# Attention passes of a hybrid layer: projecting queries and keys by tokens and transposing them, instead of projecting by features

## The chip, the cores and the metric

The kernel runs on one core of a Trainium2 chip. Five engines have queues of their own and meet through semaphores: the matrix engine (PE in the profile, with its weight loads as PEld), the vector engine (DVE), the scalar engine (ACT), GpSimd (POOL) and the sync engine (SP), which here issues the weight transfers. The metric is the device time of one execution in microseconds, the median of several.

## What is computed

One encoder layer on 256 tokens of width 2048: a projection feeds latent attention (16 heads) and a matrix-memory recurrence (8 heads), both are merged, and cross-attention and a gated feed-forward block with convolution follow. The change touches the latent attention and the convolution of the recurrence's queries and keys.

```python
def rms_norm(x, g):
    y = x * lax.rsqrt(jnp.mean(x * x, axis=-1, keepdims=True) + EPS)
    return y * g
def apply_rope(x, cos, sin):
    x1, x2 = x[..., :half], x[..., half:]
    return jnp.concatenate([x1 * cos - x2 * sin, x2 * cos + x1 * sin], axis=-1)
...
    q = (rms_norm(z_qa, g_qa) @ w_qb).reshape(b, s, 16, 128 + 64)
    kv = (rms_norm(z_kv, g_kva) @ w_kvb).reshape(b, s, 16, 128 + 128)
    q_nope = rms_norm(q[..., :128], g_qn_nope)
    q_pe = apply_rope(rms_norm(q[..., 128:], g_qn_pe), cos, sin)
    k_nope = rms_norm(kv[..., :128], g_kn_nope)
    v = kv[..., 128:]
    k_pe = apply_rope(rms_norm(z_kpe, g_kn_pe), cos, sin)     # one for all heads
    sc = (q_nope @ k_nope.T + q_pe @ k_pe.T) * scale          # causal by chunks of 64
    out = softmax(sc) @ v
...
    qk = silu(causal_dwconv(concat([zq, zk]), conv_qk))       # four taps
```

## The kernel before

All weights come as one stream of tiles of 128 x 1024 f32, through four slots (`w_raw`, `w_hi`, `w_lo`). For each tile SP transfers it, ACT copies it to a rounded `w_hi` (L730), DVE subtracts to get `w_lo` (L1205), and every product is three matmuls: high x high, high x low, low x high. `split(pos, c)` on ACT and DVE makes tile c + 4, once the matrix engine has counted tile c as used (`w_used`). The order within each engine is written out by hand.

`by_tokens` has 128 tokens as the stationary operand and 512 weight columns moving; its result has tokens on the partitions. `by_features` and `feature_tile` (L279 to L281) have 128 weight columns stationary and 256 tokens moving; their result has features on the partitions.

`mla_pass` handles a pair of heads, eight times. It takes 12 tiles: two for queries, two for keys and values, eight of a "filler", which is other work for the matrix engine while DVE and ACT prepare the attention. The filler computes the recurrence's convolution inputs in passes 0 to 2 ("qk"), its values in 3 to 6 ("v"), its output gate in 7 ("zo"). Passes 0 to 2 are one hardware loop, 3 to 6 another.

A pass on the matrix engine: queries by features into banks A0 and A3 (rotary part), keys by features into A1, values by tokens into A2. With features on the partitions, a mean of squares over features is a matmul with a constant matrix: L433 for queries, L436 for the rotary part, L441 for keys; L437 rotates halves. Those need squares from ACT (L870 to L875) and products with gains from DVE (L1362, L1365, L1369). Then fill 0, L441, fills 1 to 3, scores (L454 to L458) once `qk_ready` says that DVE has finished the keys (L1401), fills 4 and 5, transposes of the probabilities (L465), fills 6 and 7, probabilities times values (L472, L474). The inverse root is exp(-0.5 ln x) on ACT (L886 to L903, after the table load L884) and one Newton step on DVE (L1379 to L1401), on arrays 512 or 256 wide.

The convolution: ACT multiplies the last tap (`conv_first`, L861), DVE adds the other three (`conv_taps`, L1352), both from the filler's banks. DVE does this at the end of a pass, ahead of the next one.

## Time and profile before

| | us |
|---|---|
| median of 3 runs | 1811.52 |
| lowest and highest run | 1810.13, 1814.04 |
| the profiled execution | 1810.48 |
| its span | 1808.7 |
| PE busy in the span | 1776.0 |
| DVE busy | 1113.8 |
| ACT busy | 962.9 |

The span runs from the first to the last instruction; the rest of the execution's time lies around it. A row of the timeline has a start and a duration. Matmuls are pipelined, so the duration of one reaches into the next, and the cost of a stream of them is read from their starts. An entry "x4" stands for four instructions in a row.

### The profile page before, as it was taken

What the parts mean: (1) busy time and instruction counts of PE and PEld (TensorE: products, weight loads), DVE (VectorE), ACT (ScalarE), POOL (GpSimd) and SP (SyncE); (2) the same over time, 40 slices, a digit from 0 to 9 for tenths busy, and PEclk for the clock granted to TensorE, in tenths of its full rate; (3) what the DMA queues carried; (4) which work ended last, traced back from release to release, by engine and by line L of the source; (5) the groups of instructions that cost most, each with busy time, mean ns of one, the idle gap of its engine ahead of it and who ended that gap; (6) DMA issues with size and microseconds to landing.
All of it is one profiled execution on the core that took longest, in us unless ns stands there. A gap on an engine that the chain in (4) does not pass through costs nothing.

```text
span 1808.7 us, 27385 instructions
## 1 busy us (share of the span) xinstructions
PE 1776.0 (98%) x9332; PEld 1521.1 (84%) x9332; DVE 1113.8 (62%) x1473; ACT 962.9 (53%) x1294; POOL 4.6 (0%) x12
## 2 busy tenths in 40 slices
PE   5999999999999999999999999999999999999998
PEld 5899988888888888888878788888888888888887
DVE  5577676666664545454565666776666666655554
ACT  6665676765664444444555555555555555544443
POOL 0000000000000000000000000000000000000000
PEclk9999999999999999999999999999999999999999
DMA  6544444444445555555755445556555555555554
GB/s 206 184 163 152 151 162 161 162 149 145 152 161 190 193 190 191 190 190 194 261 181 185 164 151 175 185 188 188 190 189 186 187 190 190 178 194 194 190 196 151
DMA packets 88994, 325.52 MB, mean 180 GB/s; under 512 B 9920, under 2 KB 9920, under 8 KB 88176
## 3 DMA queue, kind: packets, MB, share of 16 engines
q1 hardware_dynamic: 88128, 319.85, 54.2%
q0 software_dynamic: 816, 4.98, 0.8%
q8 instruction: 33, 0.54, 0.1%
q14 instruction: 17, 0.14, 0.0%
HBM read 322.63 MB, written 2.10 MB: 180 GB/s over the span
## 4 chain that ended last, share of the span: by engine, by line
PE 95%; DVE 2%; ACT 1%; issue 1%; DMA 0%; DVEq 0%; ACTq 0%; SPq 0%
PE ps L302 18%; PE ps L271 14%; PE ps L273 14%; PE ps L272 14%; PE ps L310 9%; PE ps L705 4%; PE ps L707 4%; PE ps L706 4%; PE ps L279 2%; PE ps L281 2%; PE ps L280 2%; DVE qk L1352 1%; PE ps L454 1%; DVE w_lo L1205 1%; PE ps L455 1%
## 5 line engine op out<-in xcount | busy, mean ns | idle before, releaser
L1205 DVE TENSOR_TENSOR w_lo<-w_raw,w_hi 128x1024 fp32r<-128x1024 f32 x598 | 728.5, 1224 | 612.3 <-ACT w_hi L730 611.5
L730 ACT ACTIVATE w_hi<-w_raw 128x1024 fp32r<-128x1024 f32 x598 | 628.0, 1057 | 694.7 <-PE ps L273 353.3
L302 PE MATMUL ps<-u,w_hi 128*128 128x512 f32 x1408 | 353.3, 392 | 0.0
L302 PEld LDWEIGHTS ps<-u,w_hi 128*128 128x128 f32 x1408 | 253.0, 189 | 45.0
L271 PE MATMUL ps<-w_hi,u 128*128 128x512 f32 x608 | 243.0, 400 | 0.0
L273 PE MATMUL ps<-w_hi,u 128*128 128x512 f32 x608 | 236.8, 390 | 0.0
L272 PE MATMUL ps<-w_lo,u 128*128 128x512 f32 x608 | 236.8, 389 | 0.0
L310 PEld LDWEIGHTS ps<-u,w_lo 128*128 128x128 f32 x1408 | 192.1, 190 | 13.7
L310 PE MATMUL ps<-u,w_lo 128*128 128x256 f32 x1408 | 196.3, 282 | 0.0
L705 PE MATMUL ps<-w_hi,h_st 128*128 128x512 f32 x352 | 137.7, 391 | 2.1 <-DVE w_lo L1205 2.1
L271 PEld LDWEIGHTS ps<-w_hi,u 128*128 128x128 f32 x608 | 114.2, 188 | 28.1 <-issue 4.6
L707 PE MATMUL ps<-w_hi,h_st 128*128 128x512 f32 x352 | 137.7, 391 | 0.0
L706 PE MATMUL ps<-w_lo,h_st 128*128 128x512 f32 x352 | 137.4, 390 | 0.0
L273 PEld LDWEIGHTS ps<-w_hi,u 128*128 128x128 f32 x608 | 114.2, 188 | 24.2
L272 PEld LDWEIGHTS ps<-w_lo,u 128*128 128x128 f32 x608 | 114.3, 188 | 23.8 <-issue 1.2
L279 PE MATMUL ps<-u,w_hi 128*128 128x256 f32 x272 | 80.0, 294 | 2.5 <-DVE u L1220 2.5
L705 PEld LDWEIGHTS ps<-w_hi,h_st 128*128 128x128 f32 x352 | 66.5, 189 | 16.1 <-issue 2.5
L706 PEld LDWEIGHTS ps<-w_lo,h_st 128*128 128x128 f32 x352 | 66.5, 189 | 14.0
L707 PEld LDWEIGHTS ps<-w_hi,h_st 128*128 128x128 f32 x352 | 66.3, 188 | 14.0
L281 PE MATMUL ps<-u,w_lo 128*128 128x256 f32 x272 | 77.7, 286 | 0.0
L280 PE MATMUL ps<-u,w_hi 128*128 128x256 f32 x272 | 77.6, 285 | 0.0
L279 PEld LDWEIGHTS ps<-u,w_hi 128*128 128x128 f32 x272 | 52.9, 194 | 3.9 <-DVE u L1220 2.7
(340 smaller groups left out, 2326.5 us busy)
## 6 DMA issues: line engine op xcount, KB each, us to landing
w_raw<-in_stream SPq DMA_DIRECT2D x602, 512.0 KB, 3.4
x_tok<-in_x SPq DMA_DIRECT2D x2, 1024.0 KB, 6.6
mem_tok<-in_mem POOLq DMA_DIRECT2D x2, 1024.0 KB, 6.9
x_tok<-in_x POOLq DMA_DIRECT2D x2, 1024.0 KB, 7.4
out<-x_tok SPq DMA_DIRECT2D x8, 256.0 KB, 3.3
mats<-in_mats POOLq DMA_DIRECT2D x1, 320.0 KB, 8.2
cols<-in_cols POOLq DMA_DIRECT2D x1, 257.0 KB, 7.2
gq<-in_positions POOLq DMA_DIRECT2D x1, 128.0 KB, 9.9
```

The lines of the kernel that those rows point to most:

```text
L271: pe.matmul(o, a_hi, b_hi, start=(kc == 0), stop=False)
L272: pe.matmul(o, a_hi, b_lo, start=False, stop=False)
L273: mm = pe.matmul(o, a_lo, b_hi, start=False, stop=(kc == last_kc))
L279: pe.matmul(o, w_hi[:, s, lo:hi], a_hi, start=first, stop=False, skip_group_check=True)
L281: return pe.matmul(o, w_lo[:, s, lo:hi], a_hi, start=False, stop=last, skip_group_check=True)
L302: mm = pe.matmul(ps[:, bank + m, :], w_hi[:, s, lo:lo + P], act[:, kc, :, :].rearrange("p h t -> p (h t)"), start=(kc == 0), stop=(kc == K ...
L310: mm = pe.matmul(ps[:, bank + m, T:2 * T], w_lo[:, s, lo:lo + P], act[:, kc, 0, :], start=False, stop=False)
L705: pe.matmul(o, a_hi, b_hi, start=(first and kc == 0), stop=False)
L706: pe.matmul(o, a_hi, b_lo, start=False, stop=False)
L707: mm = pe.matmul(o, a_lo, b_hi, start=False, stop=(last and kc == 3))
L730: act.activation(w_hi[:, s, :], w_raw[:, s, :], ACT.Copy).then_inc(hi_made, 1)
L1205: TTo(w_lo[:, s, :], w_raw[:, s, :], w_hi[:, s, :].bitcast(F32), ALU.subtract).then_inc(lo_made, 1)
```

## The change

- Queries (with their rotary part, 384 columns for two heads) and keys with values (512 columns) are projected by tokens: `tokens`, into banks A0, A1 and A2, A3.
- The means of squares are now over the free axis: ACT squares, DVE reduces to 12 numbers per partition (`m_rms`), ACT takes ln and exp of those, DVE makes the Newton step on them (`inverse_root`) and multiplies the results in by token. L433, L436, L437 and L441 go.
- The rotation is done on DVE with cosine and sine by token (`cos_g`, `sin_g`), that carry the gain of the rotary queries. These tables are transposed once, ahead of the passes, by four transposes on PE.
- Queries, rotary part and keys are then transposed on PE (4, 2 and 4 transposes), and copied from PSUM by ACT (`gq`, `gp`) and by DVE (`gk`, with the product of both gains, `g_qk`). Scores go to banks A3 and A1, transposed probabilities to A0 and A2.
- The taps of chunk i run in pass i, one tap each behind splits 8, 9 and 10, and the qk filler alternates between two pairs of banks (`qk_bank`).
- The loop over passes 0 to 2 is written out; on DVE passes 0 to 3 are.

The diff, cut to its core (declarations of tiles and the constant columns are left out):

```diff
+        cos_t, sin_t = (q_tok[:, t, :, :].rearrange("p h d -> p (h d)") for t in range(TT))
+        m_rms, y_rms, r_rms = tiny[:, 0:12], tiny[:, 12:24], tiny[:, 40:52]
...
+        def qk_bank(i):
+            return GEMM + 2 * (i % 2)
...
+                if c == 2:
+                    pe.wait_ge(sem("rope_g"), 2)
+                    for i in range(2):
+                        for t in range(TT):
+                            at = (2 * i + t) * ROPE
+                            mm = pe.transpose(ps[:, ATT + 1, at:at + ROPE], gq[0:ROPE, i, t * P:(t + 1) * P],
+                                              ident[0:ROPE, 0:ROPE])
+                    mm.then_inc(sem("rope_T"), 1)
...
-                by_features(pos, G_QK + c, u, 2 * c, GEMM)
+                by_features(pos, G_QK + c, u, 2 * c, qk_bank(0))
...
+                def tokens(c, act, kc0, bank, width):
+                    sl = pos.slot(c)
                     pe.wait_ge(lo_made, pos.n(c) + 1)
                     for k in range(2):
-                        kc = 2 * c + k
-                        for h in range(2):
-                            feature_tile(ps[:, A0, h * T:(h + 1) * T], s, k * BLK + h * P, k * BLK + (h + 1) * P,
-                                         qa_t, kc, kc == 0 and h == 0, kc == LC - 1)
-                        mm = feature_tile(ps[:, A3, 0:T], s, k * BLK + 2 * P, k * BLK + 3 * P, qa_t, kc, kc == 0,
-                                          kc == LC - 1)
+                        kc = kc0 + k
+                        for t in range(TT):
+                            a_hi, a_lo = (act[:, kc, half, t * P:(t + 1) * P] for half in (0, 1))
+                            b_hi, b_lo = (w[:, sl, k * BLK:k * BLK + width] for w in (w_hi, w_lo))
+                            o = ps[:, bank + t, 0:width]
+                            pe.matmul(o, a_hi, b_hi, start=(kc == 0), stop=False)
+                            pe.matmul(o, a_hi, b_lo, start=False, stop=False)
+                            mm = pe.matmul(o, a_lo, b_hi, start=False, stop=(kc == LC - 1))
                     mm.then_inc(w_used, 1)
...
+                A0, A1, A2, A3 = ATT, ATT + 1, ATT + 2, ATT + 3
+                tokens(0, qa_t, 0, A0, 384)
+                tokens(1, qa_t, 2, A0, 384)
                 pe.wait_ge(sem("ya_lo"), it + 1)
...
-                pe.wait_ge(sem("gq_made"), it + 1)
-                pe.matmul(ps[:, A0, :], mean_nope, sq_q[:].rearrange("p h t -> p (h t)"), start=True, stop=True
-                          ).then_inc(sem("ms_q"), 1)
-                pe.wait_ge(sem("gp_made"), it + 1)
-                pe.matmul(ps[:, A3, 0:T], mean_pe, sq_p[:], start=True, stop=True)
-                pe.matmul(ps[:, A3, T:2 * T], rot, gp[:], start=True, stop=True, skip_group_check=True
-                          ).then_inc(sem("ms_p"), 1)
+                tokens(2, kv_t, 0, A2, BLK)
+                tokens(3, kv_t, 2, A2, BLK)
                 fill(0)
-                pe.wait_ge(sem("gk_made"), it + 1)
-                pe.matmul(ps[:, A1, :], mean_nope, sq_k[:].rearrange("p h t -> p (h t)"), start=True, stop=True
-                          ).then_inc(sem("ms_k"), 1)
+
+                pe.wait_ge(sem("mla_tok"), 4 * it + 1)
+                for h in range(2):
+                    for t in range(TT):
+                        mm = pe.transpose(ps[:, A0, h * T + t * P:h * T + (t + 1) * P], q_tok[:, t, h, :], ident)
+                mm.then_inc(sem("mla_T"), 1)
                 fill(1)
                 fill(2)
+                pe.wait_ge(sem("mla_tok"), 4 * it + 3)
+                for t in range(TT):
+                    mm = pe.transpose(ps[:, A1, t * P:(t + 1) * P], pe_tok[:, t, :, :].rearrange("p h d -> p (h d)"),
+                                      ident)
+                mm.then_inc(sem("mla_T"), 1)
+                pe.wait_ge(sem("mla_tok"), 4 * it + 4)
+                pe.wait_ge(sem("v_made"), it + 1)
+                for h in range(2):
+                    for t in range(TT):
+                        mm = pe.transpose(ps[:, A2, h * T + t * P:h * T + (t + 1) * P], k_tok[:, t, h, :], ident)
+                mm.then_inc(sem("mla_T"), 1)
                 fill(3)
 
-                pe.wait_ge(sem("qk_ready"), it + 1)
+                scores, probs_t = (A3, A1), (A0, A2)
+                pe.wait_ge(sem("gq_made"), 2 * it + 2)
+                pe.wait_ge(sem("gk_made"), it + 1)
...
-            with pe.Fori(0, 3) as j:
-                mla_pass(Pos(G_MLA, j, MLA_PER), j, "qk")
+            for j in range(3):
+                mla_pass(Pos(G_MLA + j * MLA_PER), j, "qk")
...
-                act.activation(sq_q[:].rearrange("p h t -> p (h t)"), ps[:, ATT, :], ACT.Square
-                               ).then_inc(sem("sqq_made"), 1)
-                act.activation(sq_p[:], ps[:, ATT + 3, 0:T], ACT.Square).then_inc(sem("sqp_made"), 1)
+                act.activation(prt[:], ps[:, ATT:ATT + 2, 0:384], ACT.Square).then_inc(sem("sqq_made"), 1)
+                act.preload_act_table_set("natural_log_exp_and_others")
+                m, y = (by_token(a) for a in (m_rms, y_rms))
                 split(pos, 2)
+                act.wait_ge(sem("ms_made"), 3 * it + 2)
+                act.activation(y[:, :, 0:4], m[:, :, 0:4], ACT.Ln).then_inc(sem("rms_ln"), 1)
+                act.wait_ge(sem("rms_ln"), 2 * it + 1)
+                act.activation(y[:, :, 0:4], y[:, :, 0:4], ACT.Exp, scale=-0.5).then_inc(sem("rms_y"), 1)
                 split(pos, 3)
-                act.activation(sq_k[:].rearrange("p h t -> p (h t)"), ps[:, ATT + 1, :], ACT.Square
-                               ).then_inc(sem("sqk_made"), 1)
-                act.activation(v_pair[:].rearrange("p t h d -> p (t h d)"), ps[:, ATT + 2, :], ACT.Copy
-                               ).then_inc(sem("v_made"), 1)
-
-
-                eps = col("eps")
-                yq, yk = (b[:].rearrange("p h t -> p (h t)") for b in (sq_q, sq_k))
-                inv = sem("inv_rms")
-                act.preload_act_table_set("natural_log_exp_and_others")
-                act.wait_ge(sem("ms_q"), it + 1)
-                act.activation(yq, ps[:, ATT, :], ACT.Ln, bias=eps).then_inc(inv, 1)
-                act.wait_ge(sem("ms_p"), it + 1)
-                act.activation(sq_p[:], ps[:, ATT + 3, 0:T], ACT.Ln, bias=eps).then_inc(inv, 1)
-                act.wait_ge(inv, 9 * it + 1)
-                act.activation(yq, yq, ACT.Exp, scale=-0.5).then_inc(inv, 1)
-                act.wait_ge(inv, 9 * it + 2)
-                act.activation(sq_p[:], sq_p[:], ACT.Exp, scale=-0.5).then_inc(inv, 1)
-                act.wait_ge(inv, 9 * it + 3)
-                act.activation(y2_q, yq, ACT.Square, scale=HALF_ROOT).then_inc(inv, 1)
-                act.wait_ge(inv, 9 * it + 4)
-                act.activation(y2_p, sq_p[:], ACT.Square, scale=HALF_ROOT).then_inc(inv, 1)
+                act.activation(pr[:, :, 0:T], ps[:, ATT + 2:ATT + 4, 0:T], ACT.Square).then_inc(sem("sqk_made"), 1)
+                act.activation(v_pair[:], heads(ps[:, ATT + 2:ATT + 4, T:2 * T]), ACT.Copy).then_inc(sem("v_made"), 1)
+                act.wait_ge(sem("ms_made"), 3 * it + 3)
+                act.activation(y[:, :, 4:6], m[:, :, 4:6], ACT.Ln).then_inc(sem("rms_ln"), 1)
+                act.wait_ge(sem("rms_ln"), 2 * it + 2)
+                act.activation(y[:, :, 4:6], y[:, :, 4:6], ACT.Exp, scale=-0.5).then_inc(sem("rms_y"), 1)
                 split(pos, 4)
-                act.wait_ge(sem("ms_k"), it + 1)
-                act.activation(yk, ps[:, ATT + 1, :], ACT.Ln, bias=eps).then_inc(inv, 1)
-                act.wait_ge(inv, 9 * it + 7)
-                act.activation(yk, yk, ACT.Exp, scale=-0.5).then_inc(inv, 1)
-                act.wait_ge(inv, 9 * it + 8)
-                act.activation(y2_k, yk, ACT.Square, scale=HALF_ROOT).then_inc(inv, 1)
+                act.wait_ge(sem("mla_T"), 3 * it + 1)
+                act.activation(gq[:].rearrange("p h t -> p (h t)"), ps[:, ATT, :], ACT.Copy).then_inc(sem("gq_made"), 1)
                 split(pos, 5)
                 split(pos, 6)
+                act.wait_ge(sem("mla_T"), 3 * it + 2)
+                act.activation(gp[:], ps[:, ATT + 1, 0:T], ACT.Copy).then_inc(sem("gq_made"), 1)
...
+            def conv_tap(i, tap):
                 dve.wait_ge(sem("cv_first"), 4 * i + 4)
-                for tap in (2, 1, 0):
-                    lag = 3 - tap
-                    if tap < 2:
-                        dve.wait_ge(sem("cv_taps"), 12 * i + 4 * (2 - tap))
-                    for m in range(4):
-                        row = 4 * i + m
-                        dst = (qk[:, row, lag:T] if isinstance(i, int) else
-                               qk[:, bass.ds(row, 1), lag:T].rearrange("p o t -> p (o t)"))
-                        STT(dst, ps[:, GEMM + m // 2, (m % 2) * T:(m % 2 + 1) * T - lag],
-                            dcol("conv_qk", 16 * i + (4 * m + tap)), dst, ALU.mult, ALU.add
-                            ).then_inc(sem("cv_taps"), 1)
-
-            conv_taps(0)
-
-            def mla_pass(pos, it, filler):
...
+            def mla_pass(pos, it, taps=None):
                 split(pos, 0)
                 split(pos, 1)
+                rp, n = sem("rp"), 13 * it
+                m, y, r = (by_token(a) for a in (m_rms, y_rms, r_rms))
+
+                def rms(lo, width):
+                    return r[:, :, lo:lo + 2].unsqueeze(3).broadcast_to([P, TT, 2, width])
+
+                def inverse_root(lo, hi, k):
+
+                    TTo(r[:, :, lo:hi], y[:, :, lo:hi], y[:, :, lo:hi], ALU.mult).then_inc(rp, 1)
+                    dve.wait_ge(rp, n + k)
+                    STT(r[:, :, lo:hi], r[:, :, lo:hi], -0.5, m[:, :, lo:hi], ALU.mult, ALU.mult).then_inc(rp, 1)
+                    dve.wait_ge(rp, n + k + 1)
+                    STT(r[:, :, lo:hi], r[:, :, lo:hi], 1.5, y[:, :, lo:hi], ALU.add, ALU.mult).then_inc(rp, 1)
+                    dve.wait_ge(rp, n + k + 2)
+
                 dve.wait_ge(sem("sqq_made"), it + 1)
-                TS(gq[:].rearrange("p h t -> p (h t)"), ps[:, ATT, :], col("g_qn_nope"), None, ALU.mult
-                   ).then_inc(sem("gq_made"), 1)
-                dve.wait_ge(sem("sqp_made"), it + 1)
-                TS(gp[:], ps[:, ATT + 3, 0:T], col("g_qn_pe"), None, ALU.mult).then_inc(sem("gp_made"), 1)
+                dve.tensor_reduce(m[:, :, 0:2], heads(prt[:, :, 0:T]), AX_X, ALU.add).then_inc(rp, 1)
+                dve.tensor_reduce(m[:, :, 2:4], heads(prt[:, :, T:384]), AX_X, ALU.add).then_inc(rp, 1)
+                dve.wait_ge(rp, n + 2)
+                TS(m[:, :, 0:2], m[:, :, 0:2], 1.0 / NOPE, EPS, ALU.mult, ALU.add).then_inc(sem("ms_made"), 1)
+                TS(m[:, :, 2:4], m[:, :, 2:4], 1.0 / ROPE, EPS, ALU.mult, ALU.add).then_inc(sem("ms_made"), 1)
                 split(pos, 2)
+                dve.wait_ge(sem("rms_y"), 2 * it + 1)
+                inverse_root(0, 4, 3)
+                TTo(pe_n[:], heads(ps[:, ATT:ATT + 2, T:384]), rms(2, ROPE), ALU.mult).then_inc(rp, 1)
+                TTo(q_tok[:], heads(ps[:, ATT:ATT + 2, 0:T]), rms(0, P), ALU.mult).then_inc(sem("mla_tok"), 1)
                 split(pos, 3)
                 dve.wait_ge(sem("sqk_made"), it + 1)
-                TS(gk[:].rearrange("p h t -> p (h t)"), ps[:, ATT + 1, :], col("g_kn_nope"), None, ALU.mult
+                dve.tensor_reduce(m[:, :, 4:6], heads(pr[:, :, 0:T]), AX_X, ALU.add).then_inc(rp, 1)
+                dve.wait_ge(rp, n + 7)
+                TS(m[:, :, 4:6], m[:, :, 4:6], 1.0 / NOPE, EPS, ALU.mult, ALU.add).then_inc(sem("ms_made"), 1)
+
+                half = ROPE // 2
+                TTo(pe_tok[:], pe_n[:], cos_g[:].unsqueeze(2).broadcast_to([P, TT, 2, ROPE]), ALU.mult
+                    ).then_inc(rp, 1)
+                for lo, other in ((0, half), (half, 0)):
+                    TTo(pe_b[:, :, :, lo:lo + half], pe_n[:, :, :, other:other + half],
+                        sin_g[:, :, lo:lo + half].unsqueeze(2).broadcast_to([P, TT, 2, half]), ALU.mult
+                        ).then_inc(rp, 1)
+                dve.wait_ge(rp, n + 10)
+                for lo, op in ((0, ALU.subtract), (half, ALU.add)):
+                    TTo(pe_tok[:, :, :, lo:lo + half], pe_tok[:, :, :, lo:lo + half], pe_b[:, :, :, lo:lo + half], op
+                        ).then_inc(sem("mla_tok"), 1)
+                split(pos, 4)
+                dve.wait_ge(sem("rms_y"), 2 * it + 2)
+                inverse_root(4, 6, 11)
+                TTo(k_tok[:], heads(ps[:, ATT + 2:ATT + 4, 0:T]), rms(4, P), ALU.mult).then_inc(sem("mla_tok"), 1)
+                split(pos, 5)
+                split(pos, 6)
+                dve.wait_ge(sem("mla_T"), 3 * it + 3)
+                TS(gk[:].rearrange("p h t -> p (h t)"), ps[:, ATT + 2, :], g_qk, None, ALU.mult
                    ).then_inc(sem("gk_made"), 1)
...
                 split(pos, 8)
+                if taps is not None:
+                    conv_tap(taps, 2)
                 split(pos, 9)
+                if taps is not None:
+                    conv_tap(taps, 1)
                 dve.wait_ge(sem("pT"), 2 * it + 2)
                 dve.wait_ge(sem("pt_1"), it + 1)
                 dve.tensor_copy(prt[:, 0, :], ps[:, ATT, 0:384]).then_inc(sem("pt_ready"), 2)
                 split(pos, 10)
+                if taps is not None:
+                    conv_tap(taps, 0)
...
-                if filler == "qk":
-                    conv_taps(it + 1)
-
+
+            dve.wait_ge(sem("tables"), 4)
+            for j in range(4):
+                mla_pass(Pos(G_MLA + j * MLA_PER), j, taps=j)
             with dve.Fori(0, 3) as j:
-                mla_pass(Pos(G_MLA, j, MLA_PER), j, "qk")
-            with dve.Fori(0, 4) as j:
-                mla_pass(Pos(G_MLA + 3 * MLA_PER, j, MLA_PER), j + 3, "v")
-            mla_pass(Pos(G_MLA + 7 * MLA_PER), 7, "zo")
+                mla_pass(Pos(G_MLA + 4 * MLA_PER, j, MLA_PER), j + 4)
...
```

## Rows read from the trace of the kernel before

**Rows 1.** PE row of the page's part 1: busy us (share of the span) xinstructions.

```profile
PE 1776.0 (98%) x9332; PEld 1521.1 (84%) x9332; DVE 1113.8 (62%) x1473; ACT 962.9 (53%) x1294; POOL 4.6 (0%) x12
```

**Rows 2.** Table of stretches: us, busy us of PE, PEld, DVE, ACT, POOL, PEclk, DMA share, GB/s.

```profile
184.50:225.90 41.40, 40.65 (x319) 38.90 (x318) 30.33 (x51) 25.20 (x42) 0.00 (x0) 1.00 0.46 151
346.50:386.00 39.50, 39.50 (x223) 33.85 (x223) 25.68 (x39) 26.98 (x42) 0.00 (x0) 1.00 0.47 159
537.00:822.00 285.00, 285.00 (x1273) 236.36 (x1272) 142.82 (x130) 122.50 (x129) 0.00 (x0) 1.00 0.59 192
```

**Rows 3.** Timeline, PE: first matmul of passes 5 and 6 (start us, us, engine line op).

```profile
306.70 0.36 PE L279 MATMUL ps<-qa_t,w_hi 128*128 128x256 f32 x1
...
346.36 0.36 PE L279 MATMUL ps<-qa_t,w_hi 128*128 128x256 f32 x1
```

**Rows 4.** Waits: engine, line, waited for, us in total, times, longest.

```profile
PE ps L433 <- DVE gq L1362: 2.9, 4, 0.8
...
PEld ps L454 <- DVE gk L1401: 1.1, 4, 0.3
```

**Rows 5.** Timeline, PE: first and last of 36 matmuls of 256 columns, of 22 of 512.

```profile
101.64 0.28 PE L279 MATMUL ps<-qa_t,w_hi 128*128 128x256 f32 x1
...
105.84 0.28 PE L281 MATMUL ps<-qa_t,w_lo 128*128 128x256 f32 x1
...
540.06 0.39 PE L271 MATMUL ps<-w_hi,y_a 128*128 128x512 f32 x1
...
544.82 0.39 PE L271 MATMUL ps<-w_hi,y_a 128*128 128x512 f32 x1
```

**Rows 6.** Timeline, PE, of a v pass: the mean and rotation matmuls and what follows.

```profile
277.20 1.02 PE L433 MATMUL ps<-sq_q,mats 128*128 128x512 f32 x2
278.05 0.59 PE L436 MATMUL ps<-sq_p,mats 128*128 128x256 f32 x2
...
279.15 0.40 PE L272 MATMUL ps<-w_lo,u 128*128 128x512 f32 x1
...
281.67 1.02 PE L441 MATMUL ps<-sq_k,mats 128*128 128x512 f32 x2
...
282.77 0.39 PE L272 MATMUL ps<-w_lo,u 128*128 128x512 f32 x1
```

**Rows 7.** Timeline, PE, of a v pass: transposes of probabilities, then the filler's second matmul.

```profile
299.35 0.82 PE L465 MATMUL ps<-mats,pr 128*128 128x128 f32 x6
...
300.24 0.39 PE L272 MATMUL ps<-w_lo,u 128*128 128x512 f32 x1
```

**Rows 8.** Timeline, all engines: a tile's last matmul, ACT's split of it, DVE's half.

```profile
126.52 0.28 PE L281 MATMUL ps<-u,w_lo 128*128 128x256 f32 x1
...
126.83 1.06 ACT L730 ACTIVATE w_hi<-w_raw 128x1024 fp32r<-128x1024 f32 x1 [1.82 <-PE ps L281]
...
127.92 1.23 DVE L1205 TENSOR_TENSOR w_lo<-w_raw,w_hi 128x1024 fp32r<-128x1024 f32 x1 [1.46 <-ACT w_hi L730]
```

**Rows 9.** Groups by line and shape: xcount, busy us, mean ns, idle before, releaser.

```profile
L884 ACT ACT_TABLE_LOAD x8 | 10.3, 1283 | 0.1
L826 ACT ACTIVATE tiny<-tiny 128x2 f32<-128x2 f32 x2 | 0.4, 204 | 0.2 <-DVE tiny L1316 0.2
...
L1408 DVE TENSOR_REDUCE tiny<-ps 128x1 f32<-128x256 f32 x16 | 6.6, 414 | 0.0
L1429 DVE TENSOR_TENSOR y_a<-ps,y_a 128x512 f32 x7 | 4.8, 692 | 4.2 <-ACT y_a L935 4.2
L1379 DVE TENSOR_TENSOR gp<-gp,cos_t 128x256 f32<-128x256 f32 x8 | 3.3, 417 | 0.0
L1411 DVE TENSOR_SCALAR tiny<-tiny 128x4 f32<-128x4 f32 x8 | 1.4, 170 | 0.3
```

**Rows 10.** Timeline, DVE: four taps of a convolution in one entry.

```profile
187.54 1.65 DVE L1352 SCALAR_TENSOR_TENSOR qk<-ps,cols,qk 128x255 f32 x4
```

**Rows 11.** Groups by line and shape: the slowest 256-wide DVE operation.

```profile
L1309 DVE RECIPROCAL kpx<-kpx 64x256 f32<-64x256 f32 x1 | 1.7, 1744 | 0.7 <-ACT kpx L815 0.7
```

127 lines of the change are left out of this document (54 added, 73 removed).

## The prediction

> **What bounds the kernel now.** I read the page first: the matrix engine is busy 98% of the span [rows 1]. The stretch table says the same of the place that changes. The first of the eight attention passes begins at 101.64 us [rows 5]. In a pass with the qk filler (184.50 to 225.90) the matrix engine idles 0.75 us of 41.4, while DVE is busy 30.3 and ACT 25.2; in one with the v filler (346.50 to 386.00) it never idles, DVE is busy 25.7 of 39.5 and ACT 27.0; the granted clock is 1.00, the 2.4 GHz level, in both [rows 2]. The weight stream doesn't bound a pass: it moves 151 to 159 GB/s there, and 192 GB/s in the merge stage where the matrix engine still has no idle time [rows 2]. So a pass is worth what its matmuls cost, plus the waits in front of them. Between two v passes lie 346.36 - 306.70 = 39.66 us [rows 3].
>
> Two waits exist. The mean matmul L433 waited 2.9 us in 4 passes for DVE's copy L1362 (0, 1, 2 and 3, those that have convolution taps ahead of them), and the weight load of the scores, L454, 1.1 us in 4 others for the last step of the keys, L1401 [rows 4].
>
> **How matmuls are priced.** A record is longer than the step to the next one, so I price by starts. A pass's 36 query matmuls of 256 columns make 35 steps from 101.64 to 105.84, 0.12 each; in the merge stage matmuls of 512 columns make 21 steps from 540.06 to 544.82, 0.227 each [rows 5]. That is 0.107 us for 256 more columns, or 0.42 ns a column, and 13 ns fixed. A 384-column row, which the trace doesn't have, lies between these ends, and on that line it costs 0.173.
>
> **The change part by part, per pass.**
>
> Queries: before, 4 chunks x 3 tiles x 3 matmuls = 36 of 256 columns, 4.31 us. After, 4 x 2 token halves x 3 = 24 of 384 columns, 24 x 0.173 = 4.16. Saved 0.15 (ends: 24 x 0.12 = 2.9 and 24 x 0.227 = 5.4; I take the line because both ends lie on one slope).
>
> Keys and values: before 48 of 256 columns, 5.75. After 24 of 512, 5.44. Saved 0.31.
>
> Removed: the mean and rotation matmuls L433, L436, L437. From 277.20 to the point where the filler is in step again (279.15 - 0.23 = 278.92) is 1.72; L441 takes 281.67 to 282.77 - 0.23, so 0.87 [rows 6]. Together 2.59.
>
> Added: 4 transposes of queries in one place, 2 of the rotary part and 4 of keys in another. Six transposes of probabilities take from 299.35 to 300.24 - 0.23 = 300.01, 0.66 with the change of kind at the end [rows 7]; that is about 0.095 each and 0.09 for the change. So 0.47 + (6: 0.66), plus their waits if any: 1.13.
>
> Net work: 0.15 + 0.31 + 2.59 - 1.13 = 1.92, times 8 = 15.4 us.
>
> Waits that go: L433's. Its 2.9 is counted from the modelled end of the record before, 0.28 - 0.12 = 0.16 after the step, so 3.5 for 4 passes. In its place stands the wait for the queries (below). L454's four waits of 1.1 in all: 0.9 if the walk below holds.
>
> Added ahead of the passes: 4 small transposes of the tables (0.47, at most 0.66 by the same row), two small DVE and two ACT instructions beside matmuls. 0.5 us.
>
> Sum: 15.4 + 3.5 + 0.9 - 0.5 = 19.3 us.
>
> **What is late next: a walk through the queues.** The new work on DVE and ACT is hidden only if four waits hold. I take full record durations. From a tile's last matmul step (126.64) the split on ACT starts after 0.19 and takes 1.06, DVE's half starts 0.03 later and takes 1.23 [rows 8]. Small instructions: 0.17 on DVE (0.21 with the hop to the next), 0.20 on ACT; 256 wide on DVE 0.42, 512 wide 0.69, 128 wide between these and the small one, I take 0.29; a 256-wide reduce 0.41, so I estimate 0.67 for 512 (bounds: 0.41 and twice it); the table load 1.28 [rows 9]. ACT's 768-wide Square lies under the 1.06 of a 1024-wide split; I take 0.8. Time 0 is a v pass's first matmul; tiles end at 2.08, 4.16, 6.88, 9.60.
>
> First wait (queries, behind fill 0, matrix engine there at 9.60 + 2.73 = 12.3): ACT splits tile 1 until 5.4, squares until 6.2, loads the table until 7.5, splits tile 2 until 8.6. DVE reduces until 7.75, two small ones until 8.1, its half of the split until 9.8; the logarithm and exponential are done at 9.0. Three small steps, 10.45; rotary part, 10.9; queries scaled, 11.6. It holds by 0.7. Queued behind a late DVE here: its half of the split of tile 3, wanted only at fill 3.
>
> Second wait (keys, there at 12.3 + 0.47 + 5.46 = 18.25): DVE half of split 3 until 12.8, reduce and mean 13.7, ACT 14.15, split 4 until 15.2; the five rotation steps fill DVE's time (0.42 + 4 x 0.29) until 15.3, its half 16.5, three small steps and the keys scaled, 17.85. It holds by 0.4.
>
> Third wait (scores, there at 18.25 + 0.66 + 2.73 = 21.65): tile 6 is free at 18.25, ACT until 19.5, DVE until 20.75, the copy with the gain 0.7, 21.45. It holds by 0.2, the thinnest. With the qk filler, whose tiles last 2.88, each slack is larger by 0.15 to 0.5.
>
> Fourth wait (probabilities transposed and copied): in the first four passes DVE now has taps between its splits, 1.65 for four [rows 10]. From the transposes of the probabilities: split 9 on DVE ends at 0.19 + 1.06 + 1.23 = 2.5, tap 4.1, copy 4.7; the matrix engine wants it after 0.66 and two fillers, 6.1 or more. Hidden. In exchange the 5 us of taps that stood between one pass and the next, behind which L1362 and two splits were queued, are gone; the double filler banks let them wait. Unrolling three turns puts nothing on the path: a new pass's first matmul takes 0.36 against 0.28 [rows 3], so there is no pause to win either.
>
> ACT's table load now stands ahead of split 2 and so ahead of the queries' scale; before it stood behind the last split that anybody waited for. Its row shows 1.28 [rows 9], and with that the queries are 0.7 early. A rule of the Trainium skill speaks against the change here (ScalarE: Activation LUTs, "What ACT_TABLE_LOAD costs"): a switch to another set costs the load and a drain, 2.66 us in all, which as an estimate would make the queries 0.7 late in each pass and the time some 5 us longer. I follow the row; the rule's mechanism is rival B.
>
> **Against the runs shown.** The profiled execution took 1810.5, its span 1808.7; 1.8 lies around the span and stays. 1810.5 - 19.3 = 1791.2. The median of the runs, 1811.5, is 1.0 above that execution, so the same sum gives 1792.2. I forecast 1792.
>
> **The rivals.**
> A. The walk is too kind: the small dependent steps take longer, and each of the three thin waits fails by a few tenths. For: the slacks are 0.7, 0.4 and 0.2, from a chain of some 15 hops, and 0.4 is less than the reduce's own uncertainty. Against: I took full records where neighbours overlap. Price, if they fail by 0.2, 0.3 and 0.5: 1.0 a pass, 8 us: 1800.
> B. ACT stands still beside its table load for as long again as the load takes, 1.28. The queries come at 11.6 + 1.28 = 12.9, 0.6 after the matrix engine: 8 x 0.6 = 5 us, 1797. For: work is now queued on both sides of the load. Against: the load's row has 0.1 us of idle time for 8 loads [rows 9]. (The skill's page named above would have 1.38 for this pause.)
> C. Slower than before: DVE's products with a repeated scale (a broadcast operand in a four-dimensional pattern) run at a rate that no product here shows. The slowest 256-wide operation of the trace is the reciprocal L1309, 1.74 us [rows 11], against 0.42. If the four wide products ran so (two of 256, two of 512), the queries would come 1.3 + 2.8 = 4.1 later and miss by 3.4, the keys again by about 3.7: 7 a pass, 56 us. It decides from 19.3 / 8 = 2.4 of lateness a pass, beyond the slacks. Against: L1379 and L1429 do the same arithmetic at 0.42 and 0.69.
> D. The change does its work but the time stays: the weights arrive too late for a shorter pass. 12 x 0.52 MB in 37.6 us is 167 GB/s; the merge stage has 192 [rows 2]. Time 1808 to 1811.
>
> **How the numbers follow.** Forecast as summed (1790 to 1794, the ends being L454's wait and the 384-column row off by 0.01): 0.62. A, with anything from 2 to 10 us lost: 0.22. B: 0.08. C: 0.03. D: 0.02. More gained than summed, down to 1787 (DVE and ACT lighter than thought elsewhere): 0.03. The range takes in B and nearly all of A, 1788 to 1801. A measurement of this kernel tells 0.2%, 3.6 us, from no change: faster 0.95, same 0.02, slower 0.03.
>
> **What would show it.** A v pass 37.5 us from first matmul to first matmul, a qk pass 38.7. No idle time before the query transposes, the key transposes or the scores; 384-column matmuls 0.173 apart. DVE's product for q_tok done 0.7 before its transposes start. Wrong if a pass gets a wait "from DVE q_tok", "k_tok" or "gk" over 0.3, or if ACT stands still after its table load.

## The result and the profile after

| | before | after |
|---|---|---|
| median of 4 runs, us | 1812.76 | 1793.36 |
| lowest and highest run | 1810.13, 1814.04 | 1790.04, 1796.12 |
| the profiled execution | 1810.48 | 1790.04 |
| its span | 1808.7 | 1788.2 |

The ratio is 0.9894, with a 95% interval of 0.9873 to 0.9915: the changed kernel is 1.1% faster, by 19.4 us on the medians. It was forecast at 1792. One execution of e8 below took 3195.03 us at a mean granted clock of 0.738, and no number here is read from it.

The page's first part of the kernel after, which answers to [rows 1]:

```profile
PE 1758.9 (98%) x9064; PEld 1505.9 (84%) x9064; DVE 1105.1 (62%) x1524; ACT 935.0 (52%) x1261; POOL 4.6 (0%) x12
```

The matrix engine's share is the same 98%: it is busy 17.1 us less, and most of the gain is that. The other two engines are no fuller than they were.

The table of stretches of the kernel after, columns as in [rows 2]: one v pass, all eight passes, and the down projection that ends the program.

```profile
331.64:369.32 37.68, 37.68 (x191) 32.09 (x190) 24.53 (x45) 24.10 (x39) 0.00 (x0) 1.00 0.52 167
...
102.33:406.98 304.65, 304.65 (x1794) 272.27 (x1793) 214.30 (x407) 181.07 (x292) 0.00 (x0) 1.00 0.51 166
...
1541.90:1788.20 246.30, 239.75 (x1057) 197.91 (x1055) 129.29 (x144) 105.05 (x130) 0.00 (x0) 1.00 0.60 185
```

The same two long stretches of the kernel before:

```profile
101.64:425.72 324.08, 321.23 (x2066) 287.48 (x2065) 223.80 (x359) 209.55 (x327) 0.00 (x0) 1.00 0.48 156
...
1560.70:1808.70 248.00, 241.37 (x1057) 199.03 (x1055) 129.29 (x144) 105.04 (x130) 0.00 (x0) 0.99 0.56 184
```

The first two columns tell the story. In the kernel after, length and PE's busy time are equal over all eight passes (304.65 and 304.65): nothing that the change added leaves the matrix engine idle. The passes went from 324.08 to 304.65, 19.4 us. By passes, from first matmul to first matmul:

| pass | 0 | 1 | 2 | 3 | 4 | 5 | 6 |
|---|---|---|---|---|---|---|---|
| before, us | 41.43 | 41.70 | 41.69 | 40.58 | 39.66 | 39.66 | 39.65 |
| after, us | 38.66 | 38.78 | 38.78 | 37.69 | 37.70 | 37.70 | 37.68 |
| gained | 2.77 | 2.92 | 2.91 | 2.89 | 1.96 | 1.96 | 1.97 |

Passes 4 to 6 had no convolution taps ahead of them, so 1.96 is what the new matrix work is worth, with at most one short wait; passes 0 to 3 gained about 0.9 more each. The first pass begins 0.69 later (102.33 against 101.64), which leaves 18.7 to 18.8. The down projection begins 18.8 us earlier (1541.90 against 1560.70) and there the difference should stay; but that stretch, in which no line was changed, took 1.7 us less in this execution, with a granted clock of 1.00 instead of 0.99. So 18.8 of the 20.5 us between the two spans are the change's.

The new matmuls, from the timeline of PE in the v pass that begins at 293.94 (rows as in [rows 3]):

```profile
293.94 0.42 PE L429 MATMUL ps<-w_hi,qa_t 128*128 128x384 f32 x1
294.20 0.34 PE L430 MATMUL ps<-w_lo,qa_t 128*128 128x384 f32 x1
...
298.01 0.33 PE L431 MATMUL ps<-w_hi,qa_t 128*128 128x384 f32 x1
...
303.67 0.39 PE L283 MATMUL ps<-w_hi,u 128*128 128x512 f32 x1
...
306.39 0.60 PE L445 MATMUL ps<-mats,q_tok 128*128 128x128 f32 x4
...
312.32 0.38 PE L451 MATMUL ps<-mats,pe_tok 128*128 128x128 f32 x2
312.54 0.60 PE L458 MATMUL ps<-mats,k_tok 128*128 128x128 f32 x4
...
315.49 0.40 PE L285 MATMUL ps<-w_hi,u 128*128 128x512 f32 x1
315.72 0.39 PE L471 MATMUL ps<-gk,gq 128*128 128x128 f32 x2
```

From 294.20 to 298.01 are 22 steps of 384 columns, 0.173 each. The filler begins at 303.67, 9.73 after the pass did. And DVE's side, the three results that those transposes and the scores wait for:

```profile
304.63 0.68 DVE L1396 TENSOR_TENSOR q_tok<-ps,tiny 128x512 f32<-128x512 f32 x1
...
310.43 0.69 DVE L1417 TENSOR_TENSOR k_tok<-ps,tiny 128x512 f32<-128x512 f32 x1
...
314.76 0.74 DVE L1421 TENSOR_SCALAR gk<-ps,tiny 128x512 f32<-128x512 f32 x1
```

Adding start and duration and comparing with the PE rows gives the slack of each wait: queries ready at 305.31 for transposes at 306.39, 1.08; keys at 311.12 for 312.54 (the rotary part goes first, at 312.32), 1.2 to 1.4; the keys with their gain at 315.50 for scores at 315.72, 0.22. These are distances from the end of a record; where a wait is made to fail, in e1, e3 and e4, the matmul starts 0.05 to 0.11 behind that end, so what can really be lost before the matrix engine stops is smaller by as much.

### The profile page after: what moved, and what is told of

Read it like the earlier page. It is cut to its first block, busy times and chain, and to the rows that moved or that the text cites. A ratio compares the mean times of both kernels' runs of the same rounds, so it can differ in the third digit from the quotient of the medians.

```text
span 1788.2 us, 26617 instructions
## 1 busy us (share of the span) xinstructions
PE 1758.9 (98%) x9064; PEld 1505.9 (84%) x9064; DVE 1105.1 (62%) x1524; ACT 935.0 (52%) x1261; POOL 4.6 (0%) x12
## 4 chain that ended last, share of the span: by engine, by line
PE 97%; DVE 1%; ACT 1%; DMA 0%; issue 0%; SPq 0%; DVEq 0%; ACTq 0%
PE ps L314 18%; PE ps L283 14%; PE ps L285 14%; PE ps L284 14%; PE ps L322 9%; PE ps L722 4%; PE ps L724 4%; PE ps L723 4%; PE ps L291 2%; PE ps L292 2%; PE ps L293 2%; PE ps L430 1%; PE ps L431 1%; PE ps L429 1%; PE ps L471 1%; PE ps L472 1%
```

## Experiments

In e1 to e8 lengths of passes are taken as in the table above, from each kernel's own profile. The kernel before ran beside them with medians of 1812.14, 1811.28 and 1813.86, one for each chip; each ratio is against the one beside it.

### Where the extra 0.9 us of passes 0 to 3 comes from: the taps

The theory says that DVE's block of taps between two passes made L433 wait, and that the token version needs the taps spread even more. Two kernels: the change without its spreading, and the spreading without the rest.

Kernel after, taps back in a block:

```diff
                 split(pos, 8)
-                if taps is not None:
-                    conv_tap(taps, 2)
                 split(pos, 9)
-                if taps is not None:
-                    conv_tap(taps, 1)
...
                 split(pos, 10)
-                if taps is not None:
-                    conv_tap(taps, 0)
                 split(pos, 11)
...
                     y_a[:, pair_rows(it), 0, :].bitcast(F32), ALU.subtract).then_inc(sem("ya_lo"), 1)
+                if taps is not None:
+                    for tap in (2, 1, 0):
+                        conv_tap(taps, tap)
...
+            for tap in (2, 1, 0):
+                conv_tap(0, tap)
             for j in range(4):
-                mla_pass(Pos(G_MLA + j * MLA_PER), j, taps=j)
+                mla_pass(Pos(G_MLA + j * MLA_PER), j, taps=j + 1 if j < 3 else None)
```

> The changed kernel, but with a chunk's three taps in one block again, at the end of the pass before (and chunk 0's ahead of pass 0); the double banks stay. Theory (the first wait, for the queries, has about 1.1 us of slack, and DVE's order sets it): DVE enters the pass about 5.2 us late, its queue ahead of the queries' scale is two splits, two reduces and a third split, so q_tok ends some 14.1 us after the pass's first matmul where the matrix engine comes at 12.5: about 1.6 us of idle time before the query transposes in passes 0 to 3, 6.4 us in all; about 1798 to 1800, with the passes' stretch 6 us longer than the changed kernel's. Rival 1 (the taps cost what they cost before, 3.5 us): 1797 with 0.9 a pass. Rival 2 (the taps were never on the path, their spreading is idle): no change, no idle time before the transposes.

Measured: 1799.29 (1797.78 to 1799.55), ratio to the kernel before 0.9927 [0.9908, 0.9947]. Passes 0 to 3 take 40.43, 40.23, 40.22 and 39.26, which is 6.2 us more than in the kernel after; passes 4 to 6 are unchanged (37.68, 37.66, 37.70). Two DVE rows of this kernel, of the pass that begins at 142.61, and its wait (columns as in [rows 4]):

```profile
145.28 5.14 DVE L1364 SCALAR_TENSOR_TENSOR qk<-ps,cols,qk 128x255 f32<-128x255 f32 x12
...
155.87 0.68 DVE L1396 TENSOR_TENSOR q_tok<-ps,tiny 128x512 f32<-128x512 f32 x1
...
PE ps L445 <- DVE q_tok L1396: 5.3, 4, 1.5
```

The twelve taps hold DVE for 5.14 us; everything behind them comes later, and q_tok is finished 13.94 after the pass began. The transposes start 0.06 later, at 14.00; in a qk pass of the kernel after they start at 12.63 (153.62 in the pass from 140.99). The wait has moved from L433 to L445, and is now longer than it was before the change.

Kernel before, with the spreading alone:

```diff
+        def qk_bank(i):
+            return GEMM + 2 * (i % 2)
...
-            def conv_taps(i):
+            def conv_tap(i, tap):
...
                 split(pos, 8)
+                if taps is not None:
+                    conv_tap(taps, 2)
                 split(pos, 9)
+                if taps is not None:
+                    conv_tap(taps, 1)
...
                 split(pos, 10)
+                if taps is not None:
+                    conv_tap(taps, 0)
                 split(pos, 11)
...
-                if filler == "qk":
-                    conv_taps(it + 1)
```

> The kernel before with only the taps spread behind splits 8, 9 and 10, the filler's banks alternating and the first three passes written out; queries and keys by features as before. Theory (the waits of the mean matmul are the taps' doing and nothing else's): they vanish, passes 0 to 2 last 40.7 us instead of 41.7, the stretch of eight passes is 3.5 to 3.9 us shorter, the time 1808 to 1809 against 1812. Rival (the waits move to the next place, the scores' wait for the keys, since DVE is as full as before): the mean matmul's wait goes and one of the same size appears before the scores; no change.

Measured: 1809.15 (1805.08 to 1811.19), ratio 0.9982 [0.9971, 0.9992]. Passes 0 to 3 take 40.59, 40.67, 40.67 and 39.61, 3.86 us less together; the others are unchanged. The mean matmul (L436 here, L433 before) in this kernel, and then in the kernel before:

```profile
152.46 0.28 PE L432 MATMUL ps<-w_hi,kv_t 128*128 128x256 f32 x1
152.58 1.02 PE L436 MATMUL ps<-sq_q,mats 128*128 128x512 f32 x2
153.44 0.59 PE L439 MATMUL ps<-sq_p,mats 128*128 128x256 f32 x2
```

```profile
153.10 0.28 PE L429 MATMUL ps<-w_hi,kv_t 128*128 128x256 f32 x1
154.15 1.12 PE L433 MATMUL ps<-sq_q,mats 128*128 128x512 f32 x2 [0.77 <-DVE gq L1362]
155.11 0.59 PE L436 MATMUL ps<-sq_p,mats 128*128 128x256 f32 x2
```

With the taps spread, one step of 0.12 and no gap; before, 1.05 from start to start, so 0.93 of wait, and then 0.96 to the next record instead of 0.86. The late pair itself runs 0.10 longer. Together that is 1.03, which is what this pass gained. That is why four waits with 2.9 in the waits' list are worth 3.9. This kernel also has its first loops written out, but that isn't the cause: pass 3, which stands in a loop of the matrix engine in both kernels, gained 0.97.

This kernel also shows the matrix work bare. Its passes 0 to 2 have no wait left, and the kernel after is shorter there by 1.93, 1.89 and 1.89: 1.90 a pass is what the projections, means and transposes are worth. In passes 3 to 6, where this kernel's scores have their short wait, it is 1.92, 1.99, 1.93 and 1.98, so by this comparison that wait costs about 0.05.

The two kernels together give the parts: by the passes, the taps are worth 3.9 us on the kernel before and 6.2 on the changed one (the medians differ by 3.0 and 5.9); the rest of the change is worth 12.9 with the taps in a block (1812.14 - 1799.29) and 15.8 with them spread (1809.15 - 1793.36, from runs on two chips).

### Does ACT stand still beside a table load?

In the prediction this was rival B, a pause of 1.28, as long as the load itself. The Trainium skill (ScalarE: Activation LUTs, "What ACT_TABLE_LOAD costs") would have 1.38. Two more loads, of another set and back, are put behind the first: if each brings a pause with it, it shows between them.

```diff
                 act.preload_act_table_set("natural_log_exp_and_others")
+                act.preload_act_table_set("exp_and_others")
+                act.preload_act_table_set("natural_log_exp_and_others")
```

> The changed kernel with two more table loads per pass behind the one that is there (to another set and back), so that ACT is 2 x 1.29 = 2.6 us later ahead of split 2. Theory (loads cost 1.28 each and no pause; the first wait has 1.05 to 1.15 us of slack, the others absorb): 1.5 us of idle time before the query transposes in each of 8 passes, 12 us: about 1804 to 1806. Rival 1 (each switch of sets also costs a pause of about its own length): 5.2 us later, over 4 us idle a pass, 33 us or more. Rival 2 (ACT's path to the queries has far more slack than the walk said): under 3 us in all.

Measured: 1806.84 (1803.88 to 1809.43), ratio 0.9967 [0.9956, 0.9977]; passes 40.21, 40.32, 40.32, 39.29, 39.27, 39.27, 39.26, so 1.54 to 1.60 more each and 12.5 us in all. ACT's timeline of the kernel after, in the v pass from 293.94, and of this kernel, in the same pass:

```profile
299.35 0.79 ACT L892 ACTIVATE prt<-ps 128x768 f32<-128x768 f32 x1
300.16 1.28 ACT L893 ACT_TABLE_LOAD   x1
301.45 1.06 ACT L747 ACTIVATE w_hi<-w_raw 128x1024 fp32r<-128x1024 f32 x1
```

```profile
307.61 1.28 ACT L893 ACT_TABLE_LOAD   x1
308.90 1.28 ACT L894 ACT_TABLE_LOAD   x1
310.19 1.28 ACT L895 ACT_TABLE_LOAD   x1
311.49 1.06 ACT L747 ACTIVATE w_hi<-w_raw 128x1024 fp32r<-128x1024 f32 x1
...
313.61 0.39 PE L285 MATMUL ps<-w_hi,u 128*128 128x512 f32 x1
315.39 0.33 PE L445 MATMUL ps<-mats,q_tok 128*128 128x128 f32 x1 [1.39 <-DVE q_tok L1398]
```

Each load takes 1.29 from start to start, and work starts 0.02 behind the last one's end, with work queued ahead of it and behind it. In the kernel after, the single load runs 1.28 and the split starts 0.01 behind it. Rival B falls. The Trainium skill (ScalarE: Activation LUTs, "What ACT_TABLE_LOAD costs") gives 1.28 for the load, which the rows have too, and 1.38 more for a drain, which they don't; the measurement decides. The run also measures the slack of the queries from the other side. q_tok ends at 315.34 here and the transposes start 0.05 later, so of the 1.08 the matrix engine can be kept waiting for 1.03 without loss: two loads, 2.58, less 1.03 is 1.55. The late transposes and the step behind them take 0.06 more, and 1.54 to 1.60 a pass was lost. The median is 0.8 above the upper end of what was expected.

### The thin wait: the keys in front of the scores

The slack of 0.22 was the thinnest. Two spare copies ahead of gk make it late by a known amount (the tiles that they write aren't read again in the pass).

```diff
                 dve.wait_ge(sem("mla_T"), 3 * it + 3)
+                for spare in (q_tok, k_tok):
+                    TS(spare[:].rearrange("p t h d -> p (t h d)"), ps[:, ATT + 2, :], g_qk, None, ALU.mult)
                 TS(gk[:].rearrange("p h t -> p (h t)"), ps[:, ATT + 2, :], g_qk, None, ALU.mult
```

> The changed kernel with two spare 512-wide copies on DVE (into q_tok and k_tok, which nobody reads any more at that point) ahead of the keys' copy gk, so that gk is 1.3 us later in each pass. Theory (the third wait is the thin one: gk ends 0.22 us before the scores in a v pass, 0.28 in a qk pass): 1.0 to 1.1 us of idle time before the scores in all 8 passes, 8.4 us: 1801 to 1803. Rival (the scores are held by something else, or later work makes it up, since DVE idles 1.4 us behind): the time stays, or rises by under 2 us.

Measured: 1803.49 (1801.92 to 1806.99), ratio 0.9956 [0.9944, 0.9969]; passes 39.88, 39.98, 39.99, 38.99, 38.94, 38.96, 38.96, so 1.20 to 1.30 more each, 9.9 us in all.

```profile
321.52 0.39 PE L285 MATMUL ps<-w_hi,u 128*128 128x512 f32 x1
322.11 0.74 DVE L1423 TENSOR_SCALAR gk<-ps,tiny 128x512 f32<-128x512 f32 x1
322.96 0.46 PE L471 MATMUL ps<-gk,gq 128*128 128x128 f32 x2 [1.04 <-issue]
```

Two copies hold DVE for 2 x 0.66 (320.79 to 322.11), so gk ends 1.10 after the point where the scores would have started; the pass lost 1.2 to 1.3, and not the 1.0 to 1.1 that was expected (8.4 us in all). The reason is in the rows. The scores start 0.11 after the copy's end and not at it, so half of the 0.22 was never slack: 1.32 - 0.11 = 1.21 of delay. And the first step of the late scores takes 0.29 (322.96, then 323.25) instead of 0.22, 0.07 more, of the kind of the 0.10 at L433. The wait is real, and it is thinner than the prediction and the rows above made it. The waits' list names "issue" and not DVE here; the rows show who was late.

Then the same wait given more room, by gk ahead of DVE's half of split 6, without the spare copies and with them:

```diff
                 split(pos, 5)
-                split(pos, 6)
                 dve.wait_ge(sem("mla_T"), 3 * it + 3)
                 TS(gk[:].rearrange("p h t -> p (h t)"), ps[:, ATT + 2, :], g_qk, None, ALU.mult
                    ).then_inc(sem("gk_made"), 1)
+                split(pos, 6)
                 split(pos, 7)
```

> The changed kernel with one step moved on DVE: the keys' copy gk ahead of the half of split 6, not behind it. Theory (split 6 is what makes the third wait thin, and no wait costs anything in the changed kernel): gk ends about 1.8 us before the scores instead of 0.2, split 6 ends 0.7 later and nobody waits for it; a v pass stays at 37.70 us and the time at 1793. Rival (the 0.1 us by which the weight load of the scores starts late is worth something): up to 0.1 a pass, 0.8 us, seen in the trace only.

> The same order with the two spare 512-wide copies ahead of gk that made the passes 9.9 us longer in the other order. Theory (place in the queue counts, not DVE's load): gk ends some 0.4 us before the scores, no wait, a v pass 37.7 us. Rival (DVE's added 1.3 us a pass are paid wherever they stand): 1.2 us a pass again, about 1803.

Measured: 1794.78 (1793.14 to 1794.82), ratio 0.9904 [0.9887, 0.9920], and with the copies 1795.36 (1793.58 to 1796.06), ratio 0.9908 [0.9892, 0.9925]. The passes of both are those of the kernel after (38.66, 38.78, 38.78, then 37.69 to 37.73). DVE and PE of the first, then of the second:

```profile
313.10 0.75 DVE L1420 TENSOR_SCALAR gk<-ps,tiny 128x512 f32<-128x512 f32 x1 [0.93 <-PE ps L458]
315.63 0.38 PE L471 MATMUL ps<-gk,gq 128*128 128x128 f32 x2
```

```profile
314.21 0.74 DVE L1422 TENSOR_SCALAR gk<-ps,tiny 128x512 f32<-128x512 f32 x1
315.42 0.38 PE L471 MATMUL ps<-gk,gq 128*128 128x128 f32 x2
```

The slack grows from 0.22 to 1.78 and nothing is gained, because the matrix engine wasn't waiting. In the kernel after the weight load of the scores did start 0.08 late (315.57, where steps of 0.23 would have it at 315.49); the passes of e5 are no shorter, so that costs nothing and the rival falls. Where e4 lost 9.9 us, the same copies now cost nothing, with gk 0.47 ahead of the scores. So of rival A there is nothing in the kernel after: the thinnest wait holds, and its lateness would have been seen.

### What matrix work costs, with every wait covered

Two kernels change the matrix engine's instructions and leave the waits covered. The first has the query matmuls at 512 columns; the 128 added ones are computed and not used.

```diff
-                tokens(0, qa_t, 0, A0, 384)
-                tokens(1, qa_t, 2, A0, 384)
+                tokens(0, qa_t, 0, A0, BLK)
+                tokens(1, qa_t, 2, A0, BLK)
```

> The changed kernel with the 24 query matmuls of a pass 512 columns wide instead of 384 (the last 128 columns of the weight tile and of the bank aren't used by anything). Theory (the matrix engine's columns are the pass's price, 0.42 ns each, and the waits have slack): 24 x 128 x 0.42 ns = 1.3 us a pass, 10.3 us in all, a v pass 39.0 us, the time 1803 to 1804. Rival (the engine has hidden spare time in a pass, or 384 columns already cost as much as 512): under 2 us.

Measured: 1804.92 (1801.55 to 1805.14), ratio 0.9956 [0.9939, 0.9973]; passes 39.93, 40.01, 40.02, 38.97, 38.94, 38.97, 38.97, so 1.2 to 1.3 more each and 10.1 us in all. One v pass of it in the table of stretches:

```profile
300.15:339.12 38.97, 38.97 (x192) 32.45 (x190) 24.53 (x45) 24.12 (x39) 0.00 (x0) 1.00 0.49 161
```

24 x (0.227 - 0.173) = 1.30. The time of a pass follows the columns one for one. At this width the queries by tokens (24 x 0.227 = 5.4) cost more than by features (36 x 0.12 = 4.3).

The second puts all ten transposes in one place, so that the matrix engine changes kind once less. It builds on the kernel with gk ahead of split 6.

```diff
                 fill(0)
+                fill(1)
+                fill(2)
                 pe.wait_ge(sem("mla_tok"), 4 * it + 1)
                 for h in range(2):
...
-                fill(1)
-                fill(2)
...
-                act.wait_ge(sem("mla_T"), 3 * it + 1)
-                act.activation(gq[:].rearrange("p h t -> p (h t)"), ps[:, ATT, :], ACT.Copy).then_inc(sem("gq_made"), 1)
                 split(pos, 5)
                 split(pos, 6)
+                act.wait_ge(sem("mla_T"), 3 * it + 1)
+                act.activation(gq[:].rearrange("p h t -> p (h t)"), ps[:, ATT, :], ACT.Copy).then_inc(sem("gq_made"), 1)
```

> The order of the keys' copy as in the run with gk ahead of split 6, and the four query transposes moved from behind fill 0 to those of the rotary part and the keys behind fill 2, ACT's copy of them behind split 6. Theory (only matrix work is left to save): one change of kind fewer, 0.06 to 0.1 us a pass, 0.5 to 0.8 us, below what the times can tell; the first wait is gone, DVE's product q_tok having 7 us of slack. Rival (the copies gq and gp now come too late on ACT): a wait before the scores of some tenths a pass.

The passes are read from a second set of executions of the same kernel:

> The kernel with one batch of transposes once more, for a profile at the full clock: a v pass 37.6 us against 37.70, no wait before the transposes or the scores; the time 1793 to 1796. If ACT's late copies were on the path, a wait before the scores of some tenths a pass.

Measured: 1794.12 to 1796.06 in four executions of the first set (ratio 0.9908 [0.9892, 0.9925]), and a median of 1792.84 in the second, of two (0.9884 [0.9856, 0.9913]); passes 38.70, 38.81, 38.81, 37.70, 37.65, 37.63, 37.64, within 0.07 of the kernel after either way, so ACT's later copies made no wait either.

```profile
311.73 0.60 PE L447 MATMUL ps<-mats,q_tok 128*128 128x128 f32 x4
312.17 0.38 PE L451 MATMUL ps<-mats,pe_tok 128*128 128x128 f32 x2
312.38 0.60 PE L458 MATMUL ps<-mats,k_tok 128*128 128x128 f32 x4
313.05 0.39 PE L284 MATMUL ps<-w_lo,u 128*128 128x512 f32 x1
```

The filler is in step again at 313.05 - 0.23 = 312.82, so ten transposes in one place take 1.09; in the kernel after they take 0.44 + 0.66 = 1.10 in two (306.39 to 307.06 - 0.23, and 312.32 to 313.21 - 0.23). The change of kind that the prediction put at 0.09 for each place isn't saved by joining them, so it is no fixed cost of a place, and the 0.5 to 0.8 us that was expected isn't there. Four transposes in 0.44, six in 0.66 and ten in 1.09 all lie on 0.11 for each and nothing besides. No kernel of these beats the changed one by more than the runs scatter: with every wait covered, only matrix work is left to take away.

## Why the prediction was right, by its steps

| step | predicted, us | measured | from |
|---|---|---|---|
| 384-column matmul | 0.173 | 0.173 | 294.20 to 298.01 |
| queries, keys and values, saved a pass | 0.46 | 0.43 | 10.16 to 9.73 |
| transposes added a pass | 1.13 | 1.10 | L445, L451, L458 |
| net work a pass | 1.92 | 1.90 | e2, passes 0 to 2 |
| L433's waits, all | 3.5 | 3.9 | e2 |
| L454's waits, all | 0.9 | 0.2 to 0.4 | e2, and the rows below |
| ahead of the passes | -0.5 | -0.7 (-0.3 to -0.6 in other profiles of changed kernels) | 102.33 against 101.64 |
| sum at the end of the passes | 19.3 | 18.7 to 18.8 | 425.72, 406.98 |
| slack of the queries | 0.7 | 1.08 | rows above |
| slack of the keys | 0.4 | 1.2 to 1.4 | rows above |
| slack in front of the scores | 0.2 | 0.22, of which 0.11 can be used | rows above, e4 |

The forecast held in time and in mechanism; the terms that were mis-sized are named below.

**What bounds the kernel.** "A pass is worth what its matmuls cost, plus the waits in front of them" held in every run. e7 added 1.30 of columns to a pass and the pass grew by 1.2 to 1.3; e5 moved DVE's work and nothing moved. The v pass, forecast at 37.5, takes 37.7, because the forecast took off L454's wait at its listed length; the qk pass, which never had that wait, takes 38.8 for 38.7 (the prediction's own terms, 41.7 less 1.92 and a quarter of 3.5, would have given 38.9).

**Prices by starts.** The line through 256 and 512 columns gave the 384-column price to the third digit. Had the records' durations been used (0.33 for 24 matmuls, 0.28 for 36), the queries alone would have come out 2.2 us a pass cheaper, against 0.15.

**L433.** The mechanism was right, DVE's taps ahead of the copy (e2: spreading them alone takes the wait away), and the size was 0.4 short. The term fell short at "0.28 - 0.12 = 0.16 after the step": that correction is right, and there is one more, the 0.10 by which the late pair runs longer (0.96 to the next record against 0.86).

**L454.** Mis-sized the other way. The term 0.9 counted the weight loads' waits as if the matrix engine had lost them. The kernel before, in pass 2, where that wait isn't, and in pass 4, where it is:

```profile
210.02 0.38 PE L454 MATMUL ps<-gk,gq 128*128 128x128 f32 x2
210.24 0.39 PE L455 MATMUL ps<-kpe,gp 128*128 128x128 f32 x2
...
290.48 0.39 PE L273 MATMUL ps<-w_hi,u 128*128 128x512 f32 x1
290.71 0.49 PE L454 MATMUL ps<-gk,gq 128*128 128x128 f32 x2
291.03 0.39 PE L455 MATMUL ps<-kpe,gp 128*128 128x128 f32 x2
```

In pass 4 the scores start a normal 0.23 after the filler, without idle time, and the next record follows after 0.32 instead of 0.22. So a weight load that waited 0.27 cost the matmul stream 0.10; by the passes of e2 it was 0.05. For all four that is 0.2 to 0.4. The step that failed is the one that read a wait of PEld as if it were one of PE.

**The walk.** The waits hold, and the slack of the third, the thinnest, was right to 0.02 us. The first two were 0.4 and 0.8 to 1.0 too pessimistic. DVE was earlier than the walk had it (q_tok 11.37 after the pass's start for 11.6, k_tok 17.18 for 17.85), because the walk let each record end before the next began; the rest is the matrix engine, which comes 0.13 to 0.15 later than the walk had it (12.45 for 12.3, 18.38 for 18.25). Grouped rows of the kernel after (columns: count, busy us, mean ns of one, idle time before):

```profile
L1387 DVE TENSOR_REDUCE tiny<-prt 128x4 f32<-128x512 f32 x8 | 5.4, 678 | 0.0
L1395 DVE TENSOR_TENSOR pe_n<-ps,tiny 128x256 f32<-128x256 f32 x8 | 3.4, 426 | 0.3
L1396 DVE TENSOR_TENSOR q_tok<-ps,tiny 128x512 f32<-128x512 f32 x8 | 5.4, 681 | 0.0
```

The estimates were 0.67 for the reduce and 0.42 and 0.69 for the products; those for 128 columns (0.29) and for the square (0.8) measured 289 and 793 ns. The durations were good; what was left over is that the next instruction starts about 0.08 before the record of the one before ends (the copies of e4: records of 0.75, starts 0.66 apart). The third wait has few hops (a split on each engine and one copy). There gk ended 0.11 later than forecast (21.56 for 21.45) and the scores came 0.13 later (21.78 for 21.65). The two errors cancel, so that the slack came out to 0.02 us is partly luck, and it left out the 0.11 from the copy's end to the earliest start of the scores.

**The rivals.** A, thin waits that fail: none does. What its waits would cost is shown by e1, e3 and e4, where they were made to fail, and in e3 and e4 it was the lateness, counted from 0.05 and 0.11 behind the record's end, and 0.06 to 0.07 more. B, a pause beside the table load: e3 shows none. C, slow products with a broadcast scale: 681 and 426 ns, the price of plain ones. D, weights too late: the stream moves 167 GB/s in a v pass, and no matmul of the passes waits for it.

**From the passes to the time.** That 19.3 stands beside 18.7 to 18.8 is helped by two errors of opposite sign, 0.4 too little for L433 and 0.5 to 0.7 too much for L454: the sum is better than its terms, and that part is luck. The medians differ by 19.4, the profiled executions by 20.4, the passes with what lies ahead of them by 18.8. In the two profiled executions the rest lies in the down projection, beside a clock of 0.99 against 1.00; of the medians, 0.6 is within their interval. The runs of one kernel scatter by 2 to 7 us, and part of that can be seen in single places that no edit touches. The same 16 matmuls of cross-attention in the kernel after and in e5, with the stretch around them:

```profile
1020.92 3.72 PE L670 MATMUL ps<-c_pt,cv 128*128 128x256 f32 x16 [2.19 <-DVE cv L1656]
...
1020.50:1026.50 6.00, 5.58 (x25) 4.80 (x26) 1.75 (x3) 1.19 (x2) 0.00 (x0) 1.00 0.29 87
```

```profile
1022.44 5.32 PE L670 MATMUL ps<-c_pt,cv 128*128 128x256 f32 x16 [2.19 <-DVE cv L1656]
...
1022.00:1028.00 6.00, 5.56 (x18) 4.62 (x19) 1.08 (x2) 0.80 (x2) 0.00 (x0) 0.72 0.25 87
```

3.72 against 5.32, with a granted clock of 1.00 over that stretch in the kernel after and 0.72 in e5, behind the same idle time of 2.19: 1.6 us in one place. What decides whether the clock falls there stays open.

## What to carry to other kernels

Where the matrix engine is never idle, count its columns and its waits first: here, moving a reduction from a matmul with a constant matrix to DVE paid in full, because each result was ready before its matmul came up. The slack at that point is the number to work out, and from it goes the short time between the end of the producer's record and the earliest start of the matmul (0.05 to 0.11 here). Long work of a helper engine that nobody waits for, such as the taps, belongs behind the last step that somebody waits for, cut into pieces; here that was worth more with the change (6.2 us) than without it (3.9). Price matmuls by the distance of their starts, and a wait by the start-to-start distance across it, not by the waits' list.
